# Differential-attention steps in another order, and two more dots in each neighbourhood step

## The reference

```python
mod = silu(c) @ w_ada + b_ada;  sh1, sc1, g1, sh2, sc2, g2 = split(mod, 6)
h = rms_norm(x, norm1_g) * (1 + sc1) + sh1
proj = h @ w_in                       # 8 neighbourhood heads (q, k, v), 8 differential heads
na_o = rms_norm(neighbourhood_attention(na_q, na_k, na_v, na_rpb), na_out_g)   # norm over all 8 heads
p = softmax(q_m @ k_m.T * 64 ** -0.5 + t5_bias)           # m = 0, 1: two maps a head
da_o = rms_norm((p[0] - lam * p[1]) @ v, da_subln_g) * (1 - lam_init)          # norm over one head
x = x + g1 * (concat(na_o, da_o) @ w_out)
h2 = rms_norm(x, norm2_g) * (1 + sc2) + sh2
x = x + g2 * ((silu(h2 @ w_gate) * (h2 @ w_up)) @ w_down)
out = rms_norm(x, final_g)
```

## Time and profile before

| what | us |
|---|---|
| median of 3 runs (lowest, highest) | 2411.35 (2411.27, 2412.03) |
| the profiled execution: its own time | 2412.26 |
| its span, first to last instruction | 2410.6 |
| TensorE busy | 2325.6 (96%) |
| VectorE busy | 1193.0 (49%) |
| ScalarE busy | 710.2 (29%) |
| GpSimd busy | 236.7 (10%) |
| mean granted TensorE clock | 0.99 of full speed |

### The profile page before, as it was taken

How to read it: one execution, slowest core, us unless ns; L and a number is a source line. 1 busy time by engine, 2 the same in 40 slices (tenths; PEclk the granted TensorE clock), 3 DMA queues, 4 the chain that set the end, 5 groups by cost and what they waited for, 6 DMA issues and landing times.

```text
span 2410.6 us, 29131 instructions
## 1 busy us (share of the span) xinstructions
PE 2325.6 (96%) x10276; PEld 1885.2 (78%) x10276; DVE 1193.0 (49%) x1602; ACT 710.2 (29%) x986; POOL 236.7 (10%) x211
## 2 busy tenths in 40 slices
PE   5999999999998998999999999999999999999997
PEld 3777888766676887788888888888888888888885
DVE  5886777877777898322333222233222332222234
ACT  3224333454445112322222222222222222222221
POOL 4001332200003332000000000000000000000032
PEclk9999999999999999999999999999999999999998
DMA  8886666533432984232233222233223233222233
GB/s 294 277 336 177 198 196 195 174 113 117 154 139 87 339 289 146 87 104 96 82 97 109 96 96 96 83 96 111 98 91 104 80 96 111 96 96 96 84 98 105
DMA packets 119482, 333.75 MB, mean 138 GB/s; under 512 B 11833, under 2 KB 36553, under 8 KB 118417
## 3 DMA queue, kind: packets, MB, share of 16 engines
q1 hardware_dynamic: 114706, 318.03, 39.3%
q0 software_dynamic: 3728, 15.01, 2.7%
q10 hardware_dynamic: 1008, 0.21, 0.1%
HBM read 325.55 MB, written 7.65 MB: 138 GB/s over the span
## 4 chain that ended last, share of the span: by engine, by line
PE 86%; DVE 9%; DMA 2%; ACT 2%; issue 1%; DVEq 0%; ACTq 0%; SPq 0%
PE P L433 18%; PE P L435 18%; PE P L434 18%; PE T L433 9%; PE T L434 9%; PE T L435 9%; DMA att<-in_w_ada 1%; DVE W_lo L1036 1%; DVE att L1310 1%; DVE rstd L1122 1%; PE T L496 1%; DMA adar<-in_w_ada 1%; PE S L478 1%; ACT W_hi L704 1%; DVE att L1071 1%
## 5 line engine op out<-in xcount | busy, mean ns | idle before, releaser
L433 PE MATMUL P<-H_hi,W_hi 128*128 128x512 f32 x2112 | 842.0, 399 | 26.5 <-DVE H_lo L1325 14.3
L1036 DVE TENSOR_TENSOR W_lo<-raw,W_hi 128x1024 fp32r<-128x1024 f32 (+2 forms) x416 | 474.8, 1141 | 721.7 <-ACT W_hi L704 718.3
L435 PE MATMUL P<-H_hi,W_lo 128*128 128x512 f32 x2112 | 826.6, 391 | 0.0
L434 PE MATMUL P<-H_lo,W_hi 128*128 128x512 f32 x2112 | 826.0, 391 | 0.0
L704 ACT ACTIVATE W_hi<-raw 128x1024 fp32r<-128x1024 f32 (+2 forms) x416 | 406.2, 977 | 1052.7 <-PE P L435 562.5
L433 PEld LDWEIGHTS P<-H_hi,W_hi 128*128 128x128 f32 x2112 | 398.5, 189 | 127.6 <-issue 36.6
L435 PEld LDWEIGHTS P<-H_hi,W_lo 128*128 128x128 f32 x2112 | 398.4, 189 | 85.1
L434 PEld LDWEIGHTS P<-H_lo,W_hi 128*128 128x128 f32 x2112 | 398.9, 189 | 80.2 <-issue 1.9
L434 PE MATMUL T<-F_lo,W_hi 128*128 128x512 f32 x704 | 273.9, 389 | 0.0
L433 PE MATMUL T<-F_hi,W_hi 128*128 128x512 f32 x704 | 273.9, 389 | 0.0
L435 PE MATMUL T<-F_hi,W_lo 128*128 128x512 f32 x704 | 273.9, 389 | 0.0
(11 more groups left out here) (175 smaller groups left out, 1696.6 us busy)
## 6 DMA issues: line engine op xcount, KB each, us to landing
raw<-in_w_gu SPq DMA_DIRECT2D x176, 512.0 KB, 3.2
raw<-in_w_in SPq DMA_DIRECT2D x72, 512.0 KB, 4.3
adar<-in_w_ada SPq DMA_DIRECT2D x72, 512.0 KB, 4.1
att<-in_w_ada SPq DMA_DIRECT2D x32, 1024.0 KB, 8.1
att<-in_w_ada SPq DMA_DIRECT2D x56, 512.0 KB, 5.0
raw<-in_w_down SPq DMA_DIRECT2D x64, 384.0 KB, 3.0
raw<-in_w_down SPq DMA_DIRECT2D x64, 320.0 KB, 2.9
raw<-in_w_out SPq DMA_DIRECT2D x32, 512.0 KB, 5.2
```

The costliest lines, as they stand in the source:

```text
L433: pe.matmul(bank[:, :], wh, xh, start=start, stop=False)
L434: pe.matmul(bank[:, :], wh, xl, start=False, stop=False)
L435: return pe.matmul(bank[:, :], wl, xh, start=False, stop=stop)
L1036: dve.tensor_tensor(lo[:, 0:cols], raw[:, raw_slot * PW:raw_slot * PW + cols], hi[:, 0:cols].bitcast(F32), ALU.subtract).then_inc(lo_done, 1)
```

## The change

- TensorE, neighbourhood steps: the second transpose moves one tile earlier, the first weighing one later.
- TensorE, differential steps of four pieces: all four scores stand in the first two pieces, the transposes begin in the middle of the third (in `before` at the start of the fourth), the head sum of the step's own head stands at its end. The wait for q_out before the fourth piece goes.
- ScalarE and VectorE follow: `o_square` and `o_rooted` at the step's end, `take_o` of the head before behind the softmax of this one (also in step 13).
- The neighbourhood norm is made in step 9: `all_sum` before the third piece, the root on ScalarE, the reciprocal on VectorE into a free part of X. The eight scalings go to steps 13 and 14, four in each.
- The dots: 8 in each neighbourhood step (6 before), none in steps 9 to 12 (2 before), 4 in steps 13 and 14 (8 before). The total of 72 stays.

The diff, cut:

```diff
-ADA = {"na4": (6, -6), "da4": (2, 48 - 2 * (NAH + 1)), "da6": (8, 56 - 8 * NK)}
+ADA = {"na4": (8, -8), "da6": (4, 64 - 4 * NK)}
...
+        na_rstd = X[:, (KT - 2) * S:(KT - 1) * S]
...
-                u, dots = ada_of(p, form)
+                u, dots = ada_of(p, form) if form in ADA else (0, 0)
...
                 head_piece(p, 1, 4, {0: lambda: scores(a, "na", 3), 3: lambda: turn_v(a, "na")})
                 pe.wait_ge(v_out, p)
-                head_piece(p, 2, 4, {0: lambda: turn_probs(a, 0), 2: lambda: turn_probs(a, 1),
-                                     4: lambda: (weigh(a, 0), turn_probs(a, 2)),
+                head_piece(p, 2, 4, {0: lambda: turn_probs(a, 0), 1: lambda: turn_probs(a, 1),
+                                     5: lambda: (weigh(a, 0), turn_probs(a, 2)),
                                      7: lambda: (weigh(a, 1), turn_probs(a, 3))})
-                pe.wait_ge(q_out, p + 1)
-                head_piece(p, 3, 4, {2: lambda: weigh(a, 2), 5: lambda: weigh(a, 3)})
-
-            def da_step4(p, a, prev):
+                head_piece(p, 3, 4, {3: lambda: weigh(a, 2), 5: lambda: weigh(a, 3)})
+
+            def da_step4(p, a, na_sum=False):
 
                 scores(a, "da", 0)
-                head_piece(p, 0, 4, {2: lambda: head_sum(a - 1) if prev else None, 4: lambda: scores(a, "da", 1)})
-                head_piece(p, 1, 4, {1: lambda: scores(a, "da", 2), 6: lambda: turn_v(a, "da")})
+                head_piece(p, 0, 4, {3: lambda: scores(a, "da", 1), 7: lambda: scores(a, "da", 2)})
+                head_piece(p, 1, 4, {3: lambda: scores(a, "da", 3), 5: lambda: turn_v(a, "da")})
                 pe.wait_ge(v_out, p)
-                head_piece(p, 2, 4, {0: lambda: scores(a, "da", 3)})
-                pe.wait_ge(q_out, p + 1)
-                head_piece(p, 3, 4, {0: lambda: turn_probs(a, 0), 1: lambda: turn_probs(a, 1),
-                                     3: lambda: (weigh(a, 0), turn_probs(a, 2)),
-                                     5: lambda: (weigh(a, 1), turn_probs(a, 3)), 7: lambda: weigh(a, 2)})
-                weigh(a, 3)
-
-            def da_step6(p, a, prev=False, na_sum=False):
+                if na_sum:
+                    pe.wait_ge(v_ready, a + 1)
+                    all_sum(NAH)
+                head_piece(p, 2, 4, {4: lambda: turn_probs(a, 0), 6: lambda: turn_probs(a, 1)})
+                if na_sum:
+                    pe.wait_ge(root_made, 2)
+                head_piece(p, 3, 4, {0: lambda: (weigh(a, 0), turn_probs(a, 2)),
+                                     2: lambda: (weigh(a, 1), turn_probs(a, 3)),
+                                     4: lambda: weigh(a, 2), 5: lambda: weigh(a, 3)})
+                head_sum(a)
+
+            def da_step6(p, a, final=False):
 
                 scores(a, "da", 0)
                 pe.wait_ge(v_out, p)
-                head_piece(p, 0, 6, {2: lambda: head_sum(a - 1) if prev else None, 4: lambda: scores(a, "da", 1)})
+                head_piece(p, 0, 6, at_mid(scores, a, "da", 1))
                 scores(a, "da", 2)
                 head_piece(p, 1, 6, at_mid(scores, a, "da", 3))
                 turn_v(a, "da")
                 pe.wait_ge(k_out, p)
                 head_piece(p, 2, 6)
-                if na_sum:
-                    pe.wait_ge(o_out, a)
-                    pe.wait_ge(v_ready, a + 1)
-                    all_sum(NAH)
                 turn_probs(a, 0)
                 head_piece(p, 3, 6, at_mid(turn_probs, a, 1))
...
-                if na_sum:
-                    pe.wait_ge(root_made, 2)
+                if final:
                     head_piece(p, 5, 6, {2: lambda: scores(p, "da", 0), 4: lambda: head_sum(a),
...
-            da_step4(NAH + 1, NAH, False)
+            da_step4(NAH + 1, NAH, na_sum=True)
             with pe.Fori(NAH + 2, NK) as p:
-                da_step4(p, p - 1, True)
...
                 split_head(p + 1, 0, 4)
                 take_out(p, 3, 4, Pb[1], vT, v_out, 1.0)
 
-            def da_step4(p, a, prev, following=4):
+            def da_step4(p, a, following=4, na_sum=False):
                 split_head(p, 1, 4)
                 exp(a, "da", 0)
-                if prev:
-                    o_square(a - 1)
-                    o_rooted(a - 1)
                 exp(a, "da", 1)
                 split_head(p, 2, 4)
                 exp(a, "da", 2)
+                exp(a, "da", 3)
                 take_v_high(a)
                 split_head(p, 3, 4)
-                exp(a, "da", 3)
                 take_out(p, 1, 4, Pb[0], backwards(q_hi), q_high, -q_scale("da"))
                 take_key(p)
+                if na_sum:
+                    all_root(2, NAH * P)
                 take_turned(a, 0)
                 take_turned(a, 1)
                 split_head(p + 1, 0, following)
                 take_turned(a, 2)
                 take_turned(a, 3)
+                if na_sum:
+                    act.wait_ge(rstd_made, 2)
+                o_square(a)
                 take_out(p, 3, 4, Pb[1], vT, v_out, 1.0)
-
-            def da_step6(p, a, prev=False, na_sum=False):
+                o_rooted(a)
...
-                    dve.wait_ge(kept, p)
+                    dve.wait_ge(kept, p if form == "na4" else p + (NAH + 1 - NK))
                 dve.wait_ge(ada_in[v % 2], 8 * u + 16 * (v // 2 + 1))
...
                 take_o(a, "na")
-                ada(p, "na4", 4)
-                ada(p, "na4", 5)
+                for v in range(4, 8):
+                    ada(p, "na4", v)
                 keep(p, "na4")
 
-            def da_step4(p, a, prev, following=4):
+            def da_step4(p, a, prev=True, following=4, na_norm=False):
                 bias_scores(a, "da", 0)
                 split_head(p, 1, 4)
+                bias_scores(a, "da", 1)
                 normalise(a, "da", 0)
-                bias_scores(a, "da", 1)
+                bias_scores(a, "da", 2)
                 normalise(a, "da", 1)
-                bias_scores(a, "da", 2)
                 split_head(p, 2, 4)
+                bias_scores(a, "da", 3)
+                normalise(a, "da", 2)
+                normalise(a, "da", 3)
+                take_v(a)
+                split_head(p, 3, 4)
                 if prev:
                     take_o(a - 1, "da")
-                normalise(a, "da", 2)
-                bias_scores(a, "da", 3)
-                take_v(a)
-                split_head(p, 3, 4)
-                normalise(a, "da", 3)
-                q_low(p, Pb[0], "da")
-                k_low(p, key_land)
                 turned_low(a, 0)
                 turned_low(a, 1)
+                if na_norm:
+                    dve.wait_ge(root_made, 2)
+                    dve.reciprocal(na_rstd, root[:, :]).then_inc(rstd_made, 1)
+                    dve.wait_ge(rstd_made, 2)
+                q_low(p, Pb[0], "da")
+                turned_low(a, 2)
+                k_low(p, key_land)
+                turned_low(a, 3)
                 split_head(p + 1, 0, following)
-                turned_low(a, 2)
-                turned_low(a, 3)
-                ada(p, "da4", 0)
-                ada(p, "da4", 1)
-                keep(p, "da4")
-
-            def da_step6(p, a, prev=False):
+
+            def da_step6(p, a, prev, scales):
...
+                if prev:
+                    take_o(a - 1, "da")
                 split_head(p, 4, 6)
                 turned_low(a, 0)
                 turned_low(a, 1)
-                ada(p, "da6", 2)
                 q_low(p, Pb[0], "da")
+                na_scale(scales[0])
                 split_head(p, 5, 6)
-                ada(p, "da6", 3)
+                ada(p, "da6", 0)
                 turned_low(a, 2)
                 k_low(p, Pb[1][:, :])
                 turned_low(a, 3)
-                ada(p, "da6", 4)
-                ada(p, "da6", 5)
+                ada(p, "da6", 1)
+                ada(p, "da6", 2)
                 split_head(p + 1, 0, 6)
-                ada(p, "da6", 6)
-                ada(p, "da6", 7)
+                for k in scales[1:]:
+                    na_scale(k)
+                ada(p, "da6", 3)
...
-                dve.wait_ge(o_out, a)
-                all_rstd(2)
                 turned_low(a, 1)
                 split_head(p, 5, 6)
                 turned_low(a, 2)
                 k_low(p, Pb[1][:, :])
                 turned_low(a, 3)
-                na_scale(range(0, NAH))
-                dve.wait_ge(na_scaled, NAH)
...
-            def na_scale(ks):
-                for k in ks:
-                    xk = X[:, k * S:k * S + S]
-                    dve.scalar_tensor_tensor(xk, xk, gna[:, k:k + 1], rstd[:, :], ALU.mult, ALU.mult)\
-                        .then_inc(na_scaled, 1)
+            def na_scale(k):
+                xk = X[:, k * S:k * S + S]
+                dve.scalar_tensor_tensor(xk, xk, gna[:, k:k + 1], na_rstd, ALU.mult, ALU.mult).then_inc(na_scaled, 1)
```

(53 more changed lines are left out.)

## The result

| | median (lowest to highest), us | ratio to before |
|---|---|---|
| before, in the same rounds | 2411.59 (2411.27 to 2412.03, 4 runs) | |
| changed kernel | 2439.16 (2437.91 to 2445.87, 4 runs) | 1.0121 [1.0109, 1.0134] |

A forecast was written before the change was run, and what follows sets the result against it. TensorE, working 2325.6 of 2410.6 us, was taken as the bound. Terms 22.2, 11.9, 9.0, -9.2, -7.5, -1.1, -2.85 and -0.5 sum to +21.95, giving 2433 us; range 2408 to 2445, own range 2424 to 2442.

The forecast's parts named there:

- Third scores of neighbourhood steps: In steps 2 to 8 two added dots delay bias_scores, so the third scores wait 3.8 us: +22.75.
- The clock: After the long waits of steps 2 to 9 the granted clock falls: 7 drops of 1.7 us, +11.9.
- Rival B: The waits come but the clock holds: +10, 2421 us; chance 0.10.
- rival A: In neighbourhood steps bias_scores is delayed little, since loads land before the dots: 2405 or 2389 us; chance 0.16.
- HAM oscillation: Skill section on loops that wait each round: every round can pay half rate; by it the eighth wait pays too, +1.7.
- The estimate of 3.2 us for a load: Skill's figure for a 512 KB load to the dots; by it the wait would be about 3.0, the sum 5.6 smaller.
- Step 9: Second scores wait 5.4 us; head sum, all_sum and a wait of 1.7 are added: 40.8 us, +9.0.
- Steps 10 to 12: The head sum is ready, the first weighing waits 1.25 us, each step takes 33.55: -9.2.
- Rival C: In steps 10 to 12 the first weighing waits 3 us and the clock falls: +10, 2443 us; chance 0.12.
- Steps 13 to 15: Waits, step 13's early head sum and clock loss, and step 15's all_sum go: -7.5, -1.1 and -2.85.
- VectorE has lost four dots: Step 13: scalings of two times four heads stand where the dots were, take_o after the softmax; within its -7.5.
- Behind: Behind step 15: eight scalings less, but the head sum and ScalarE's copies keep the order: -0.5.

The follow-up runs named there:

- the old dots: Changed kernel's attention order and norm in step 9, with 6 dots in a neighbourhood step, 2 in steps 9 to 12, 8 in 13 and 14: 2397.5 us.
- the dots without loads: Changed kernel with dots 6 and 7 of neighbourhood steps reading the resident condition vector, two loads a step less: 2419.43 us.
- The idle matmuls: Changed kernel with 16 or 8 matmuls, their result unread, ahead of the third scores in steps 2 to 8: 2428.33 and 2427.88 us.

## Why the prediction was right, and where a size was off

- Third scores of neighbourhood steps: a wait of 3.8 in seven steps. Right in kind and nearly in size. The waits are 3.88, 3.93, 3.45, 4.35, 4.11, 4.56 and 3.81, mean 4.0. What was missing in it is the idle 0.54 at the loop's end; a round trip 0.2 shorter than in the earlier trace rows made up for part. The prediction named steps of 34 to 35 us; they are 33.8 to 37.5, five of them above 36. That two dots and the way to their data cause it is shown by the old dots (all of the wait goes) and by the dots without loads (1.8 of it goes).
- The clock: 7 drops of 1.7, 11.9. By the trace this is the term that was mis-sized. The clock fell in six of steps 2 to 8 and in step 9, so the count holds; but by clock and length of each step the loss is 16.9 in steps 2 to 8 and 3.4 in step 9, 20.3 together. The size came from a wait of 3.3 us. Four steps of 0.91 lost 3.3 to 3.4 each, two of 0.95 lost 1.7 and 1.8, and step 8 none, after a wait of 3.81. Rival B (no clock loss) falls by these rows, rival A (small waits) by the waits. But length times clock counts too much, since in most of these steps the clock falls while TensorE still waits and executes nothing. The last 1.5 us of the wait in step 2:

```profile
254.03:255.53 1.50, 0.00 (x1) 0.00 (x1) 1.09 (x6) 0.02 (x1) 0.00 (x0) 0.58 0.16 60
```

Some 2.6 of the 16.9 us lie inside the waits. The idle matmuls, which take the drop away, give the price by experiment: the clock costs 12.6 in steps 2 to 8, where 10.2 had been counted. What remains with the full clock is 240.3 - 212.3 = 28.0 above the kernel before, where the waits had been priced at 22.75. So by this experiment the larger part of the miss in these steps, 5.3 of 7.7, belongs to the waits and what they bring with them, and 2.4 to the clock; the trace's sum alone would put it the other way round.

- The Trainium skill, "TensorE: Matmul & The Clock Gate", section "HAM oscillation": a loop with a wait in every round can pay half rate in every round. The trace agrees: six of seven steps paid, 1.7 to 3.4 us each by length and clock, and step 9 too. Not every round paid: step 8 lost nothing.
- The estimate of 3.2 us for a load by the Trainium skill ("DMA: Bandwidth & Descriptors", section "Anatomy of one DMA") is worked out from figures that the section gives for DMAs issued by GpSimd; these loads are issued by SyncE. The earlier trace rows has 3.1 for one of them, but the way from dot 5's end to dot 7's start measured 4.12 here, as the earlier trace rows had it and not as the estimate.
- Step 9: 10.7 forecast with its clock, 11.3 measured. The wait of the second scores was 5.48 (5.4 forecast), that of all_sum 1.47 (1.7); the clock lost 3.4 where 1.7 was counted, so the work was put too high by 1.
- Steps 10 to 12: right, -9.5 for -9.2, and it is the order that gains it: -9.6 with the old dots. The first weighing waits 1.00, 1.00 and 0.82 for 1.25. Rival C, which had 3 us here, is refuted.
- Steps 13 to 15: -11.6 for -11.45. The reason "VectorE has lost four dots" is confirmed: with the eight dots back these steps take 9.7 more, nearly all of the gain. It is half of the reason, for without the new order the four dots less gain only 2.6.
- Behind: -2.0 where -0.5 was priced. With the norm back in step 15, 1.75 of it goes, so it belongs to the norm's work that left step 15. Behind step 15 a wait of the scores (0.94 before, 0.93 with the norm back) is gone, and one of the transposes is 1.58 where it was 2.52 in both. The prediction's 0.5 counted neither.
- The forecast's own range of 2424 to 2442 is wider than its terms give: eight waits 1.0 shorter or 0.9 longer make about 2425 to 2440.

What stays open: which waits of 2 to 5 us bring the lower clock and for how long, and why the waits of one order differ by up to 1.5 us (the load of dot 6 or 7 lands earlier or later; its neighbours in the queue weren't varied).

## What to carry to other kernels

Work that "fits into VectorE's idle share" is priced by what stands behind it in that engine's order: here 2.4 us of dots cost 6.4 us a step (44.6 over seven), since a two-half buffer made them a round trip, the loop's first instruction frees a bank for TensorE, and the clock fell behind the wait. Four dots a step in steps 9 to 12 cost 0.4 us a step, where the next thing behind them was wanted late. When a change has parts that act in different steps, run each part alone before keeping or dropping it: here the new order won 14 us and, with the dots placed otherwise, 22. Don't add up what the parts did alone: in steps 13 to 15 they gained 1.8 and 2.6, and together 11.6.

## What the runs showed of the hardware that was not expected

- The half rate comes in two sizes, and the wait's length alone sets neither its coming nor its size: 1.7 us lost behind 3.3 (before) and 2.23 (dots without loads), 3.1 behind 4.11, 1.8 behind 4.56, none behind 3.81 and 2.29. Sixteen or eight idle matmuls in the wait kept it away in 13 of 14 steps.
- VectorE idles 0.17 to 0.56 us before the first instruction of each of seven rounds (0.54 to 0.56 in five), with the name "issue": nothing that the profile shows holds it. The row of VectorE's waits in the changed kernel, 240 to 500 us:

```profile
DVE att L1064 <- issue: 3.3, 7, 0.6
```

- The dot at 392.64 takes 2.05 us, those clear of GpSimd 1.22; the copy takes 0.17 where it had taken 1.02. GpSimd's product and sum of the head's squares run beside the long ones. The dot ahead, which starts at 391.50, before the product, takes 1.22. The two dots more moved the copy out of this, which gave 0.85 us back. That GpSimd is the cause is read from the overlap; no run moves its work. Timeline of GpSimd:

```profile
391.85 1.76 POOL L1630 TENSOR_TENSOR sq<-X 128x512 f32 x1 [2.04 <-DVE X L1112]
393.69 2.15 POOL L1632 TENSOR_TENSOR sqacc<-sqacc,sq 128x512 f32<-128x512 f32 x1
```
